# Attention steps of an encoder layer rearranged: row sums spread by DMA, output projection laid between more steps, spatial mixing and residual loads moved under attention

## The reference

```python
a = rms_norm(h, g_mix);  z = a @ w_in            # q, k, v, u, v_gmlp: 5120 columns
# differential attention: 8 heads, two components of 64, values of 128
s  = einsum('bqhcd,bkhcd->bhcqk', q, k) * 64**-0.5       # q, k with partial rotary
pr = softmax(s, axis=-1)
o  = (pr[:, :, 0] - lam * pr[:, :, 1]) @ v
o  = rms_norm(o, g_subln) * (1 - lambda_init)             # per head
# spatial gating: a 128 x 128 position matrix for each of 8 channel groups
gm = gelu(u) * (w_s @ layer_norm(gelu(v_gmlp)) + b_s)
h  = h + concat([o, gm]) @ w_out
h  = h + (silu(conv(rms_norm(h) @ w_up)[g]) * conv(...)[u]) @ w_down
h  = h + (p @ w_ple_up) * sigmoid(rms_norm(h) @ w_ple_gate)
return rms_norm(h, g_final)
```

## Time and profile before

| | us |
|---|---|
| median of 3 runs | 2069.48 (2062.49 to 2089.54) |
| the profiled execution | 2064.24 |
| its span, slowest core (core 7) | 2062.7 |
| spans of the other cores | 2053.6 to 2061.1 |
| PE busy in it | 1917.6 (93%) |
| ACT busy | 749.4 (36%) |
| DVE busy | 999.0 (48%) |
| mean granted TensorE clock | 0.984 |

### The profile page before, as it was taken

How to read it: one execution, slowest core, us unless ns; L and a number is a source line. 1 busy time by engine, 2 the same in 40 slices (tenths; PEclk the granted TensorE clock), 3 DMA queues, 4 the chain that set the end, 5 groups by cost and what they waited for, 6 DMA issues and landing times.

```text
span 2062.7 us, 31107 instructions; the slowest of 8 cores (2053.6 to 2062.7 us)
## 1 busy us (share of the span) xinstructions
PE 1917.6 (93%) x11708; PEld 1059.0 (51%) x11708; DVE 999.0 (48%) x1305; ACT 749.4 (36%) x1039; POOL 186.3 (9%) x281
## 2 busy tenths in 40 slices
PE   5988999987889999988999999999999999999994
PEld 1433455554445555545666654566654566644441
DVE  3645201254444544554566641366641366643667
ACT  4621111104887777765222210122210022233553
POOL 5600000000000000001000000000000010001000
PEclk9998999999999999999999999999999999999997
DMA  9750344366002333328644444444444464444603
GB/s 223 221 109 14 69 82 62 53 120 195 1 1 42 52 54 60 52 52 134 111 73 75 78 75 75 78 79 75 74 75 78 82 103 77 71 72 83 108 26 138
DMA packets 60371, 170.43 MB, mean 83 GB/s; under 512 B 10816, under 2 KB 15168, under 8 KB 60096
## 3 DMA queue, kind: packets, MB, share of 16 engines
q0 software_dynamic: 34992, 125.58, 36.3%
q1 hardware_dynamic: 25232, 42.86, 6.6%
HBM read 279.29 MB, written 8.39 MB: 139 GB/s over the span
## 4 chain that ended last, share of the span: by engine, by line
PE 81%; DVE 6%; ACT 5%; issue 4%; DMA 3%; SPq 1%; POOL 1%; DVEq 0%; ACTq 0%; POOLq 0%
PE ps L336 81%; ACT big L339 4%; DVE big L342 3%; DMA big<-xo 1%; SPq L559 1%; DVE big L354 1%; DVE big L345 1%; DMA big<-wup 1%; POOL big L349 1%; DVE big L351 1%; DMA big<-xa 0%; DVEq L170 0%; DMA big<-big 0%; DMA big<-posa 0%; DVE big L349 0%
## 5 line engine op out<-in xcount | busy, mean ns | idle before, releaser
L336 PE MATMUL ps<-big 128*128 128x342 bf16 (+3 forms) x11708 | 1917.6, 330 | 125.1 <-ACT big L339 51.0
L336 PEld LDWEIGHTS ps<-big 128*128 128x128 bf16 (+1 forms) x11708 | 1059.0, 98 | 982.1 <-issue 257.9
L339 ACT ACTIVATE big<-big 128x1024 f32<-128x1024 f32 (+8 forms) x547 | 423.4, 792 | 925.8 <-DVE big L342 703.0
L342 DVE TENSOR_TENSOR big<-big 128x342 f32<-128x342 f32 (+8 forms) x424 | 306.1, 735 | 224.0 <-ACT big L339 190.2
L339 ACT ACTIVATE big<-ps 128x684 bf16<-128x684 f32 (+1 forms) x432 | 294.6, 705 | 178.2 <-PE ps L336 173.0
L345 DVE SCALAR_TENSOR_TENSOR big<-big 128x1024 f32<-128x1024 f32 (+1 forms) x228 | 258.5, 1134 | 207.2 <-ACT big L339 197.6
L342 DVE TENSOR_TENSOR big<-ps,big 128x1026 f32<-128x1026 f32 (+4 forms) x239 | 210.7, 897 | 284.1 <-PE ps L336 271.0
L342 DVE TENSOR_TENSOR big<-big,ps 128x342 f32<-128x342 f32 (+1 forms) x96 | 83.1, 866 | 202.6 <-PE ps L336 201.4
L402 POOL DMA_DIRECT2D big<-wup x88 | 46.5, 528 | 539.4 <-PE ps L336 508.7
L339 ACT ACTIVATE big<-ps,big 128x512 bf16<-128x512 f32 x50 | 34.0, 686 | 159.4 <-PE ps L336 159.4
L402 POOL DMA_DIRECT2D big<-wo x48 | 25.5, 532 | 518.5 <-PE ps L336 508.9
(11 more groups left out here) (25 smaller groups left out, 64.5 us busy)
## 6 DMA issues: line engine op xcount, KB each, us to landing
big<-wup POOLq DMA_DIRECT2D x88, 512.0 KB, 5.7
big<-wo POOLq DMA_DIRECT2D x48, 512.0 KB, 5.1
big<-xa SPq DMA_DIRECT2D x32, 512.0 KB, 7.2
big<-wdn POOLq DMA_DIRECT2D x32, 480.0 KB, 5.3
big<-xo SPq DMA_DIRECT2D x16, 512.0 KB, 9.9
big<-wg POOLq DMA_DIRECT2D x16, 512.0 KB, 13.7
y<-big SPq DMA_DIRECT2D x32, 256.0 KB, 2.2
big<-wdn POOLq DMA_DIRECT2D x16, 448.0 KB, 4.9
```

Source lines behind the costliest of these rows:

```text
L336: P.op("pe", lambda e: e.matmul(out, lhsT=lhsT, rhs=rhs, start=start, stop=stop), reads=reads, writes=writes, inc=inc)
L339: P.op("act", lambda e: e.activation(out=out, in_=in_, func=func, **kw), reads=reads, writes=writes)
L342: P.op(en, lambda e: e.tensor_tensor(out=out, in0=a, in1=b, op=op), reads=reads, writes=writes)
```

## The change

What it does:

- The row sums are no longer split and summed by `sum3`. Bank 6 is copied to `SM`; its four strip rows go by DMA to the output tensor in memory (rewritten at the end), and two DMAs bring them back, each spread over the 128 partitions, to `LA` and `LB`. `post_add` adds the two (step 8), `post_ln` and `post_exp` (steps 10 and 11) run on both components at once, 684 wide, `post_o` follows at step 11. `post_b` is now at step 1 of the unit after, with `post_rs` and `post_out` at steps 3 to 5.
- `FILL` lays the same 32 matmuls of the output projection over 14 of the 16 steps. `flush_sq` takes one square at each of steps 12 and 14.
- The 16 spatial parts come at steps 3, 8 and 12 of units 0 to 5, in bank 7 only.
- The residual is loaded in pieces at step 6 of units 1 to 4, 7, 8 and 10 to 15; the last block's part of tiles 0 to 3 and the two neighbours' columns only after attention.
- At unit 23 seven slots more take weights of the output projection, in the room of keys no longer read.
- After attention tiles 0 to 3 of block 2 start without the last head (`wl(j, 0, 15)`), `hg` is filled for blocks 0 and 1 ahead (`hg_copy`). `hg`, and with it some buffers of the MLP, change places.

```diff
@@ row sums
             if kt == 15:
                 cpy(XO, ps[:, 4:6, 0:NB], [Rb[4], Rb[5]], [R_XO])
-                split3(ps[:, 6, 0:NB], [Rb[6]])
+                cpy(SM, ps[:, 6, 0:NB], [Rb[6]], [R_sm])
+                yb = y_d[0, 4 * (k // 16 % 2):4 * (k // 16 % 2) + 4, 0:NB]
+                P.dma("sp", lambda e: e.dma_start(out=yb, in_=h[0:128:32, 0, 684:1026]), DS_yb, reads=[R_sm], writes=[R_yb])
+                P.dma("sp", lambda e: e.dma_start(out=LA, in_=yb[0:2, :].partition_broadcast(128)), DS_l, reads=[R_yb], writes=[R_la])
+                P.dma("sp", lambda e: e.dma_start(out=h[:, 1:3, 684:1026], in_=yb[2:4, :].partition_broadcast(128)), DS_l, reads=[R_yb],
+                      writes=[R_lb])
+                R_la.w = R_lb.w = (DS_l.sem, DS_l.cnt)
...
-        def post_a(u, c):
...
+        def post_add(u):
+            for c in range(2):
+                tt(LA[:, c, :], LA[:, c, :], LB[c], ALU.add, [R_lb], [R_la])
...
+        def post_o(u):
+            tt(OO, XO[:, 0, :], LA[:, 0, :], ALU.mult, [R_XO, R_la], [R_oo])
+            stt(LA[:, 1, :], XO[:, 1, :], neglam, LA[:, 1, :], ALU.mult, ALU.mult, [R_XO, R_lam], [R_la])
+            tt(OO, OO, LA[:, 1, :], ALU.add, [R_la], [R_oo])
+            tt(RM, OO, OO, ALU.mult, [R_oo], [R_rm])
+            split3(RM, [R_rm])
@@ the loop
+        FILL = [0, 0, 3, 2, 2, 2, 2, 2, 3, 2, 2, 2, 2, 3, 3, 2]
...
+            if u == 23 and st == 0:
+                for i in range(7):
+                    sl = Slot(Z3 + i * 4096, True)
...
+                pump()
             if k < nstep:
                 emit_qk(k)
-            fl = 9 <= u < 24 and st in (1, 2, 3, 4, 9, 10, 11, 12)
...
+            nf = FILL[st] if 9 <= u < 24 else 0
+            fill(gen, nf - nf // 2)
+            if u < 9 and st in (3, 8, 12):
+                if sp_i[0] < 16:
+                    spatial_mm()
...
+            if u >= 2 and st == 1:
+                post_b(u - 2)
...
+            fill(gen, nf // 2)
...
-            if st in (7, 15):
-                flush_sq()
...
+            if st in (12, 14):
+                flush_sq(1)
...
+            if st == 6:
+                if 1 <= u <= 4:
+                    h_first(u - 1, gate)
...
@@ after attention
+        fill(gen, 1000)
+        post_add(23)
+        for i in range(2):
+            h_last(i, [], [R_sm, R_lb])
+        h_tail([R_sm, R_lb])
+        post_ln(23)
+        post_exp(23)
+        post_o(23)
+        flush_sq()
+        for j in range(8):
+            hg_copy(j)
+        for j in range(4):
+            wl(j, 0, 15)
+        post_b(23)
+        post_rs(23, 0)
+        post_rs(23, 1)
+        post_out(23)
...
+        for j in range(8, 16):
+            hg_copy(j)
+        for j in range(4, 6):
+            wl(j, 0, 15)
+        for j in range(6):
+            wl(j, 15, 16)
+        for j in range(6, 16):
+            wl(j, 0, 16)
```

225 lines of the change are left out of this document (129 added, 96 removed).

## The result

| | before | changed |
|---|---|---|
| median, us | 2066.05 (4 runs, 2062.49 to 2089.54) | 2131.18 (4 runs, 2128.06 to 2157.24) |
| profiled execution, us | 2064.24 | 2131.9 |
| its span, slowest core | 2062.7 (core 7) | 2130.3 (core 4) |
| spans of the other cores | 2053.6 to 2061.1 | 2113.6 to 2128.6 |
| mean granted clock | 0.984 | 0.966 |

A forecast was written before the change was run, and what follows sets the result against it. No single engine was taken to bound attention: PE's matmuls plus the scores-exponential-scores loop did, with PE waiting for spatial mixing in the q stage. Terms -20.5 + 4.4 + 9.1 + 2.2 + 4 - 8.5 = -9.3 gave 2055 us, range 2040 to 2072.

The follow-up runs named there:

- e11: e4 with the seven extra weight loads issued only after unit 23's own row sums were read; ratio 1.0195 to the kernel before.
- e12: e11 with the first eight scaled copies also behind unit 23's inverse root on ScalarE; ratio 1.0165 to the kernel before.
- e13: e11 with the seven loads waiting until the residual's last two columns had landed; ratio 1.0036 to the kernel before.
- e4: Changed kernel with unit 23's seven loads at step 8, first square at step 6, residual loads at step 10; profiled 2092.7 us against 2069.4 for the kernel before.

## What to carry to other kernels

A short transfer on the critical path has no price of its own: price it beside the heaviest load that can stand next to it, look at every transfer issued ahead of it, on any queue, and count its rows, since here each row waited for a packet of the load. Moving that load elsewhere only helps if no other small transfer stands there. Work "hidden" under another stage must be placed by the in-order queue and the PSUM bank that it passes through, not by an engine's idle time; the same mixing cost 21.5 us at steps 3, 10 and 12 and 1.6 us at steps 0 and 4. Taking away one stop shows the next in the same queue, 1.7 us here. And a short stall that returns in every unit also costs clock.

## What the runs showed of the hardware that I had not expected

- Broadcasts of 342 KB took 4.6 us in the median and 22 us from issue to use beside seven 512 KB weight loads, which themselves took 23.2; two transfers of 8 KB in rows of 8 bytes kept VectorE waiting 28.6 and 31.8 us beside them (e11, e12), and landed in 4.4 us without them (e13). The DMA engines were busy for 0.77 of unit 23, at 130 GB/s (core 4).
- While both had work, SyncE's and GpSimd's queues moved packets one for one: 1453 of mostly 8 bytes and 1454 of 4096 in 30 us (e11), 470 of 1368 and 476 of 4096 in 14 us (changed kernel).
- TensorE's granted clock fell to half after stalls of 2.8 us that came once in a unit of 21 us, in 3 to 9 stretches per core over 14 units; none of the cores had one in these units before, when the longest of PE's waits for ScalarE was 0.9 us. In e4, with stalls of 1.7 to 2.1 us there, a core had none to two. The cores of one execution differed by 10 us in these units, in step with their time at half clock.
- A write through memory and a pair of broadcasts back, with no residual load beside them, still took 6.9 us from the store's issue to the addition (587.12 to 594.02 in e4's unit 6, core 3), two fifths of the unit.
